# Decoder block on one core: the first piece of w_in loaded in two halves, its first half and half of its products moved ahead of the last two modulation pieces

## The reference

```
mod = silu(c) @ w_ada + b_ada            # 6 x 1024: shift1, scale1, gate1, shift2, scale2, gate2
h   = rms_norm(x, norm1_g) * (1 + scale1) + shift1
x   = x + gate1 * mixer_sublayer(h, w_in, ...)   # p = h @ w_in, conv branch, attention branch, gates
h   = rms_norm(x, norm2_g) * (1 + scale2) + shift2
x   = x + gate2 * moe_sublayer(h, ...)           # router, 64 experts (8 per token), a shared expert
```

## Time and profile before

| what | value |
|---|---|
| median of 3 runs | 730.31 us (727.36 to 730.33) |
| profiled execution, span | 727.8 us |
| TensorE (PE) busy | 664.3 us, 91% of the span |
| VectorE (DVE) busy | 303.3 us, 42% |
| ScalarE (ACT) busy | 168.3 us, 23% |
| mean TensorE clock granted | 0.978 |
| DMA | 225.66 MB, mean 310 GB/s |
| chain that ended last | PE 59%, DMA 34%, DVE 3%, SP queue 2%, issue 1% |

### The profile page before, as it was taken

How to read it: one execution, slowest core, us unless ns; L and a number is a source line. 1 busy time by engine, 2 the same in 40 slices (tenths; PEclk the granted TensorE clock), 3 DMA queues, 4 the chain that set the end, 5 groups by cost and what they waited for, 6 DMA issues and landing times.

```text
span 727.8 us, 10005 instructions
## 1 busy us (share of the span) xinstructions
PE 664.3 (91%) x3371; PEld 375.1 (52%) x3371; DVE 303.3 (42%) x690; ACT 168.3 (23%) x292; POOL 34.2 (5%) x61
## 2 busy tenths in 40 slices
PE   2899999999999999989998989989889898898995
PEld 0388865888886487654433433434334343343342
DVE  1247989988243477352232122222231223222224
ACT  2010134213220241122232223122222222222211
POOL 7001112000000001000000000000000000000001
PEclk9799999999999999999999999999999999999999
DMA  8998989633420006617899999999999999999971
GB/s 303 387 387 289 391 309 340 243 126 127 184 88 0 1 3 268 252 54 293 332 428 423 430 422 427 429 425 428 425 424 430 425 429 425 422 432 421 428 297 58
DMA packets 43133, 225.66 MB, mean 310 GB/s; under 512 B 3489, under 2 KB 3521, under 8 KB 29415
## 3 DMA queue, kind: packets, MB, share of 16 engines
q1 hardware_dynamic: 41528, 224.43, 76.6%
q10 hardware_dynamic: 1582, 0.94, 0.5%
HBM read 224.31 MB, written 1.05 MB: 310 GB/s over the span
## 4 chain that ended last, share of the span: by engine, by line
PE 59%; DMA 34%; DVE 3%; SPq 2%; issue 1%; ACT 0%; ACTq 0%; DVEq 0%
DMA raw<-n_w_experts_gate_up_dram 31%; PE bank L1154 16%; PE bank L1488 13%; PE bank L1437 4%; PE bank L1293 4%; PE bank L1325 4%; DMA ring<-in_w_ada_dram 3%; PE bank L1472 3%; PE bank L1182 2%; PE bank L1448 1%; PE bank L1478 1%; SPq L323 1%; PE bank L1118 1%; PE bank L1496 1%; PE bank L1105 1%
## 5 line engine op out<-in xcount | busy, mean ns | idle before, releaser
L1488 PE MATMUL bank<-raw,hT 128*32 128x512 f32 x832 | 97.9, 625 | 29.2 <-DMA raw<-n_w_experts_gate_up_dram 29.2
L1154 PE MATMUL bank<-work,ring 128*128 128x256 f32 x512 | 116.2, 384 | 1.4 <-ACT work L500 1.4
L1154 PEld LDWEIGHTS bank<-work,ring 128*128 128x128 f32 x512 | 97.3, 192 | 17.0 <-issue 2.9
L1472 PE MATMUL bank<-raw,hT 128*128 128x512 f32 x224 | 101.6, 607 | 2.8 <-ACT hT L629 2.8
L1053 DVE TENSOR_TENSOR sg<-sg,bank 128x256 f32<-128x256 f32 x27 | 11.4, 422 | 168.2 <-ACT sg L638 168.2
L1488 PEld LDWEIGHTS bank<-raw,hT 128*32 128x32 f32 x832 | 30.7, 115 | 95.3 <-issue 95.3
L1472 PEld LDWEIGHTS bank<-raw,hT 128*128 128x128 f32 x224 | 42.0, 192 | 62.1 <-issue 61.3
L1448 PE MATMUL bank<-y,ST 128*128 128x512 f32 x224 | 70.2, 435 | 2.3 <-DVE y L1062 2.3
L638 ACT ACTIVATE sg<-bank 128x256 f32<-128x256 f32 x27 | 17.1, 634 | 193.0 <-PE bank L1488 109.8
L1038 DVE TENSOR_SCALAR SI<-iota,slotm,wt 128x32 f32 (+2 forms) x108 | 30.1, 315 | 56.6 <-issue 56.6
L1448 PEld LDWEIGHTS bank<-y,ST 128*128 128x128 f32 x224 | 39.0, 189 | 25.7 <-issue 17.6
(11 more groups left out here) (279 smaller groups left out, 584.5 us busy)
## 6 DMA issues: line engine op xcount, KB each, us to landing
raw<-n_w_experts_gate_up_dram SPq DMA_DIRECT2D x53, 2048.0 KB, 16.7
raw<-in_w_experts_down_dram SPq DMA_DIRECT2D x53, 1024.0 KB, 18.5
ring<-in_w_ada_dram SPq DMA_DIRECT2D x12, 2048.0 KB, 18.5
ring<-in_w_in_dram SPq DMA_DIRECT2D x9, 2048.0 KB, 13.2
ring<-in_w_out_dram SPq DMA_DIRECT2D x2, 2048.0 KB, 8.6
ring<-in_w_attn_out_dram SPq DMA_DIRECT2D x1, 2048.0 KB, 19.0
ring<-in_w_conv_out_dram SPq DMA_DIRECT2D x1, 2048.0 KB, 7.7
ring<-in_w_shared_gate_up_dram SPq DMA_DIRECT2D x1, 2048.0 KB, 7.8
```

The costliest lines, as they stand in the source:

```text
L1154: ins = mm(b[:, kk * SEQ:(kk + 1) * SEQ], w[:, k, m * PART:(m + 1) * PART], h1T[:, k, :], start=(k == 0), stop=(k == KD - 1))
L1472: ins = mm(psU[:, :], hT[:, k, :], wg[:, k, :], start=(k == 0), stop=(k == KD - 1))
L1488: ins = mm(psU[c:c + 32, :], hT[:, k, c:c + 32], w_gu(s)[:, k, :], start=(k == 0), stop=(k == KD - 1))
```

## The change

The list `order` puts ("in", 0) at place 2, ahead of ("mod", 2) and ("mod", 3). It is loaded in two DMAs of 1 MB: slices 0 to 3 at its place (semaphore `early_in`), slices 4 to 7 right behind ("mod", 3). TensorE runs `mod_columns(0)` before `mod_piece(1)`, and after `mod_columns(1)` the first four slices of the two halves of units 0 and 1 (16 matmuls); then `mod_piece(2)`, `mod_columns(2)`, `mod_piece(3)`, `mod_columns(3)`, and then the other 16 matmuls. Each of the four partial sums has a PSUM bank of its own (`EARLY_B`). VectorE's copies are reordered to suit; ScalarE reads the gates of a unit with two instructions in place of one. By its place in the ring (n = 2) the piece shares its buffer with ("ada", 1), n = 7.

```
-        order = [("mod", 0), ("mod", 1), ("mod", 2), ("mod", 3), ("in", 0), ("ada", 0), ("in", 1), ("ada", 1), ("ada", 2),
+        order = [("mod", 0), ("mod", 1), ("in", 0), ("mod", 2), ("mod", 3), ("ada", 0), ("in", 1), ("ada", 1), ("ada", 2),
...
+        EARLY_B = [(1, 5), (2, 6)]
...
+                if n == EARLY:
+                    sp.dma_start(piece(n)[:, 0:KD // 2, :], pieces[n][:, 0:KD // 2, :]).then_inc(early_in, 16)
+                    continue
                 sp.dma_start(piece(n), pieces[n]).then_inc(piece_in[n % NBUF], 16)
+                if n == MOD[3]:
+                    sp.dma_start(piece(EARLY)[:, KD // 2:KD, :], pieces[EARLY][:, KD // 2:KD, :]).then_inc(piece_in[EARLY % NBUF], 16)
...
-                    ins = a.activation(gsig[:, 2 * u:2 * u + 2, :], ps2, ACT.Sigmoid)
+                    for kk in range(2):
+                        ins = a.activation(gsig[:, 2 * u + kk, :], bank[EARLY_B[u][kk]][:, 0:SEQ], ACT.Sigmoid)
...
             mod_row_out(0)
+            mod_column(0)
             mod_row_out(1)
-            mod_column(0)
-            mod_row_out(2)
             mod_column(1)
             h1_out(1)
+            mod_row_out(2)
+            mod_column(2)
             mod_row_out(3)
-            mod_column(2)
             mod_column(3)
             h1_out(3)
...
-            for j in range(1, 4):
-                mod_piece(j)
-                mod_columns(j - 1)
+            mod_columns(0)
+            mod_piece(1)
+            mod_columns(1)
+
+            pe.wait_ge(early_in, 16)
+            pe.wait_ge(h1T_act, 2)
+            pe.wait_ge(h1T_dve, 2)
+            for u in range(2):
+                project_in(u, (0, 1), range(0, KD // 2))
+            mod_piece(2)
+            mod_columns(2)
+            mod_piece(3)
             mod_columns(3)
             pe.wait_ge(h1T_act, 4)
             pe.wait_ge(h1T_dve, 4)
...
-                    project_in(u, (0, 1))
+                    project_in(u, (0, 1), range(KD // 2, KD) if u < 2 else range(KD))
```

More of the change, by code:

```diff
@@ L208, in hybrid_conformer_fox_moe_block @@
         (AOUT, COUT, WOUT, SHGU, SHD) = (21, 22, 23, 25, 26)
+        EARLY = order.index(("in", 0))
         MOD = [order.index(("mod", j)) for j in range(4)]
@@ L232, in hybrid_conformer_fox_moe_block @@
         piece_in = [sem(f"piece_in{i}") for i in range(NBUF)]
+        early_in = sem("early_in")
         gu_in = [sem(f"gu_in{i}") for i in range(NW)]
@@ L1139, in _, with project_in @@
                 ins.then_inc(h1T_ps, 1)
-            for j in range(1, 4):
-                mod_piece(j)
-                mod_columns(j - 1)
+            def project_in(u, halves, ks=range(KD)):
+                w = piece(UNIT_PIECE[u])
+                for kk in halves:
+                    m = 2 * (u % 2) + kk
+                    b = bank[EARLY_B[u][kk] if u < 2 else UNIT_B[u % 4] if u < 10 else M_B[u % 2]]
+                    at = 0 if u < 2 else kk * SEQ
+                    for k in ks:
+                        ins = mm(b[:, at:at + SEQ], w[:, k, m * PART:(m + 1) * PART],
+                                 h1T[:, k, :], start=(k == 0), stop=(k == KD - 1))
+                if kk == 1 and KD - 1 in ks:
+                    ins.then_inc(unit_done, 1)
+            mod_columns(0)
[9 more added lines that the diff above has]
+            mod_piece(3)
             mod_columns(3)
@@ L1145, in _ @@
             pe.wait_ge(h1T_dve, 4)
[L1147 to L1157, removed]
             def forget_and_stats():
```

## The result

| | before | changed | ratio | 95% interval |
|---|---|---|---|---|
| first measurement, median | 729.89 us (4 runs) | 738.08 us (4 runs) | 1.0093 | 1.0069 to 1.0118 |
| again, with more runs | 730.74 us (19) | 736.13 us (6) | 1.0082 | 1.0059 to 1.0106 |
| span of the profiled execution | 727.8 us | 734.5 us | | |

The ratios are not the quotients of the medians, which would be 1.0112 and 1.0074. A run's time is 1.8 us over its span, so the execution of the kernel before that was profiled (span 727.8) took about 729.6 us, close to the median. In what follows A is the end of unit 1 on TensorE; before, it is 55.3.

What follows compares the result with a forecast made beforehand. The prediction took TensorE's almost unbroken chain from 27 us to the experts as the bound. It summed -1.0 at A, unit 4 +3.2 and clock +1.96 to +5.1, taking the median from 730.3 to 735.4 us, range 730.5 to 739.

Steps and rivals of the forecast that it cites:

- the moved wait: SyncE queue: "ada" 1's load waits for units 0 and 1, holding back ("in", 2), which lands 19.6 us after A.
- clock +1.96: TensorE at unit 4: after the idle spell the clock falls to half, adding 1.96 us.
- To the early matmuls: TensorE at the start: modulation columns, piece 1 and its row copy put the first early matmul at 27.8 us.
- The early matmuls: First halves of units 0 and 1: sixteen matmuls take 6.9 us plus 1.96 for the clock, ending at 36.7.
- The modulation tail: Modulation pieces 2 and 3 wait for the early matmuls; the rest of units 0 and 1 starts at 45.4.
- A: End of unit 1 on TensorE: forecast at 54.3 us against 55.34 before, bounds 50.3 and 56.9.
- At unit 4: Unit 4 lacks weights until 73.9 against a start at 70.7 before: loss 3.2 us, plus 1.96 for the clock.
- Nothing takes it up later: Behind unit 4: the chain has no room to give back, so the 5.1 us of lateness stays.
- The first: Rival: one clock fall less, before the second half or at unit 4, with ("in", 2) still late; +3.1, 733.4 us, chance 0.25.
- The third: Rival: modulation pieces drop the clock again, A is 56.9 and the loss +7.7, 738 us; chance 0.20.
- Not slower at all: Rival: early matmuls keep TensorE at the upper clock, no fall happens and A is 50.3; 729.5 us, chance 0.07.

Runs made afterwards that it cites:

- experiment 1: Changed kernel with the piece's ring place and waits of before, so the load of "ada" 1 no longer waits for units 0 and 1; ratio to before 0.9975.
- experiment 2: Kernel before with one wait added: the load of "ada" 1 waits for units 0 and 1; ratio to before 1.0101.
- experiment 3: Changed kernel with ten matmuls whose results nothing reads, put in TensorE's two waits behind unit 3; ratio to before 1.0081.
- experiment 6: Changed kernel with the ring place and waits of before, and the sixteen early matmuls spread among the modulation pieces and columns; ratio to before 0.9951.
- experiment 7: Changed kernel with the ring place and waits of before and no early matmuls, all 32 behind the modulation pieces; ratio to before 1.0020.
- experiment 4: Changed kernel with its loads, but all 32 matmuls of units 0 and 1 behind the modulation pieces; ratio to before 1.0152.
- experiment 5: Changed kernel run again without any edit; ratio to before 1.0082.

## Why the prediction was right

The forecast was 735.4 us, +5.1 against the median before. The two medians are 738.1 and 736.1. The ratios give +6.8 (1.0093) and +6.0 (1.0082), and their intervals reach together from 4.3 to 8.6. So the forecast is on the low side. The mechanism is the one named: experiments 1 and 2 show it by taking the moved wait out of the changed kernel and by putting it alone into the one before. That the size came out as well as it did is in part luck, as the errors of the steps cancel. One line of the forecast does not add up as it stands: "-1.0 at A; unit 4 +3.2; clock +1.96; together +5.1" gives 4.2. The 3.2 is counted from where unit 4 stood before (73.9 against 70.7) and holds the 1.0 already; the sum meant is 3.2 + 1.96. Step by step:

*To the early matmuls.* Predicted 27.8, measured 27.6.

*The early matmuls.* Predicted at half clock, to 36.7. In the changed kernel's two profiles they ran at full clock, 7.1 us to 34.8; in experiments 1 and 3 they were at half clock for some 3.5 us and took 8.8 us. The term of 1.96 us was there in two profiles of four.

*The modulation tail.* Predicted 8.7 us from their end to the second half; measured 43.6 - 34.8 = 8.8. The second half had its slow start (8.8 us, predicted 8.9).

*A.* Predicted 54.3; 52.4 and 52.1 measured, by the clock of the early part.

*The moved wait.* Predicted that ("in", 2) lands 19.6 after A, between 19.0 and 20.2; measured 72.6 - 52.4 = 20.3. The upper of the two estimates (20.2, from five loads in a row) was the right one; the likeliest value was 0.7 too low, since the first load took 9.3 us from issue to use, not 8.2. Why is open. It is not that three loads were issued in a row here: behind the load with the 8.2, issued at 101.1, stood four more, the first of them issued at 101.57.

```profile
101.57 18.77 SPq L319 DMA_DIRECT2D ring<-in_w_in_dram  x4
```

The Trainium skill's fixed cost of about 2.0 us (DMA: Bandwidth & Descriptors, Anatomy of one DMA, given there for DMAs that GpSimd issues, while these are issued by SyncE) would have given A + 18.3; the trace puts three loads at 16.3 us of bytes and 4.0 besides.

*At unit 4.* Predicted a loss of 3.2 and 1.96 for the clock; measured, on the chain, 1.8 (72.64 against 70.88) and 2.7 (9.58 against 6.91). Both terms were mis-sized; their sum is 4.4, which is what the units are late, and near the 5.1. A came 1.9 us sooner than forecast and would alone have made the stall that much shorter; the landing, 0.7 later as counted from A, and the slow clock, 0.7 dearer, made up for most of it.

*Nothing takes it up later.* Right in the changed kernel. But I costed the clock as an addition to the stall, and experiment 3 shows that it mostly covers another wait: with 2.5 us of it removed, 0.6 us was gained.

*The rivals.* The first was one fall of the clock less, at +3.1. There was one less than forecast in both profiles of the changed kernel, at a place that it did not name (the early matmuls), and the units are 4.4 late, between it and the forecast. The third, that the modulation pieces run at the lower clock, did not come in the changed kernel: both took 1.9 us. Nor did it in experiments 1 and 3, where the early block itself met the fall. "Not slower at all" needed A of at most 51.1 and no fall at unit 4; the clock fell there. Its premise that the early matmuls keep the clock up came true in these two profiles up to the second half, so its chance of 0.07 rested on too firm a view of the clock.

*The part behind the scores.* The span is 6.7 longer, of which 4.5 had arisen before the fourth expert load (328.03, before 323.53). From the first scores to that load it takes 196.4 us in all nine profiles, so up to there the lateness of the scores is the whole loss.

```profile
323.53 0.33 SPq L323 DMA_DIRECT2D raw<-n_w_experts_gate_up_dram  x1
328.03 0.33 SPq L332 DMA_DIRECT2D raw<-n_w_experts_gate_up_dram  x1
```

The other 2.2 are in the part behind it, which took 404.3 us in the profile of before and 406.5 in both of the changed kernel. It also took 405.0 to 406.7 in the profiles of the other six kernels, 406.6 and 406.7 among them with the old wait (experiments 6 and 7). So these 2.2 us don't go with the moved wait; the one profile of before is at the short end. What sets the scatter was not looked into. Where the ratios lie over the 4.4 us (0.6%), it is open how much of that is scatter.

## What to carry to other kernels

In a ring of buffers, a piece's place in the order fixes two things, when it is loaded and whose load will wait for it. A piece that is moved ahead but used up late holds back the load that comes round to its buffer, and all that the queue has behind that. A load can be issued early and still keep the buffer of its late place (experiment 1 needed nothing else to turn 0.8% lost into 0.25% won). Work put in front of a critical tail should fill the tail's gaps rather than stand as a block ahead of it (experiment 6: A at 49.4 against 54.2, and the scores 2.6 us sooner). And price a slow clock or a wait only after asking what the next limit is: here 2.5 us removed were worth 0.6.

## What the runs showed that I had not expected

The same instructions at the same place of the program ran at either clock: the sixteen early matmuls, started at 27.6 to 27.7 in three profiles, took 7.14, 7.14 and 8.83 us. What TensorE did ahead of them was the same in all three, so the clock of a short stretch can't be forecast from one trace of it. In the third the granted clock fell 1.3 us after the block had begun, in the midst of dense work.

The first 2 MB load behind the queue's standstill was used 9.2 to 9.7 us after its issue (the changed kernel, experiments 2 to 5), against 8.2 for "ada" 7 in the trace of before, which also had further loads directly behind it. One thing differs: the DMA engines had moved almost nothing for 3 us or more before the issue at A, and for 0.5 us before that of "ada" 7. Whether that is the cause was not tested.
